# A gathered-expert decoder layer: the gates' exponential and its division one step later in each unit

## The reference, cut to what matters

```python
s1, i1 = lax.top_k(scores[:, :, :, 0, :], PEER_TOPK)
s2, i2 = lax.top_k(scores[:, :, :, 1, :], PEER_TOPK)
cand = (s1[..., :, None] + s2[..., None, :]).reshape(B, S, PEER_HEADS, PEER_TOPK * PEER_TOPK)
top_s, top_c = lax.top_k(cand, PEER_TOPK)
...
gates = jax.nn.softmax(top_s, axis=-1).astype(x.dtype)
...
ue = jnp.take(u_tab, idb, axis=0)
h = jnp.einsum('thkd,td->thk', ue, xb)
act = gb * jax.nn.gelu(h, approximate=False)
ve = jnp.take(v_tab, idb, axis=0)
return jnp.einsum('thk,thkd->td', act, ve)
```

## Time and profile before

| | us |
|---|---|
| median of 3 runs | 1428.41 |
| lowest and highest | 1425.42, 1432.09 |
| the profiled execution | 1430.31 |
| its span, first to last instruction | 1428.6 |
| busy: PE, DVE, ACT, POOL | 1132.4, 1078.3, 936.5, 562.6 |
| granted TensorE clock, mean share of full | 0.889 |

### The profile page before, as it was taken

The page is one execution under the profiler, slowest core; times in us unless marked ns, Lnnn a source line. Parts: engine busy times, 40 slices in busy tenths (PEclk is TensorE's granted clock), DMA queues, the critical chain, the costliest instruction groups (busy, mean ns, idle before and its releaser), DMA issues.

```text
span 1428.6 us, 19360 instructions
## 1 busy us (share of the span) xinstructions
PE 1132.4 (79%) x6804; PEld 882.6 (62%) x6804; DVE 1078.3 (75%) x2602; ACT 936.5 (66%) x1613; POOL 562.6 (39%) x535
## 2 busy tenths in 40 slices
PE   9999999988689877796646988877658776776666
PEld 4567777666676666675645557755556565555555
DVE  1488777668778886688757668888887788878867
ACT  2245677679878888766636666567666766667563
POOL 1044344334544344445324334444334343434341
PEclk9999999999889989899778987888788888888778
DMA  9799999999999999999999999999999999999994
GB/s 356 277 387 423 419 426 394 425 423 426 414 426 404 426 422 424 426 426 421 427 428 426 425 426 409 416 408 426 427 427 404 425 427 426 428 426 427 426 425 148
DMA packets 89787, 584.06 MB, mean 409 GB/s; under 512 B 9709, under 2 KB 15253, under 8 KB 22490
## 3 DMA queue, kind: packets, MB, share of 16 engines
q0 software_dynamic: 74288, 536.90, 89.9%
q1 hardware_dynamic: 15402, 45.92, 8.2%
HBM read 580.69 MB, written 2.10 MB: 408 GB/s over the span
## 4 chain that ended last, share of the span: by engine, by line
DMA 47%; PE 22%; DVE 18%; issue 7%; ACT 4%; POOL 2%; POOLq 0%; DVEq 0%; ACTq 0%
DMA arena<-in_uv,ids 47%; DVE arena L1819 9%; PE ps L1187 6%; PE ps L1082 2%; PE ps L1006 2%; PE ps L872 2%; POOL arena L658 2%; ACT arena L1445 2%; PE ps L702 1%; PE ps L692 1%; PE ps L685 1%; ACT actv L1438 1%; PE ps L949 0%; PE ps L942 0%; PE ps L769 0%
## 5 line engine op out<-in xcount | busy, mean ns | idle before, releaser
L658 POOL DMA_INDIRECT arena<-in_uv,ids x512 | 549.1, 1073 | 802.9 <-DVE hid L1819 527.8
L1187 PE MATMUL ps<-ident,arena 128*128 128x128 f32 x4076 | 613.9, 310 | 278.2 <-ACT arena L1445 277.1
L1187 PEld LDWEIGHTS ps<-ident,arena 128*128 128x128 f32 x4076 | 535.3, 160 | 378.2 <-ACT arena L1445 336.8
L1819 DVE CUSTOM_DVE_ANT_1 arena<-arena 128x1024 f32<-128x1024 f32 x384 | 468.4, 1224 | 195.4 <-DMA arena<-in_uv,ids 192.2
L1445 ACT ACTIVATE arena<-arena,actv 128x1024 f32<-128x1024 f32 x511 | 554.2, 1131 | 0.2
L1435 ACT ACTIVATE gel<-hid 128x2 f32<-128x2 f32 (+1 forms) x257 | 52.1, 203 | 378.6 <-DVE hid L1819 378.1
L1819 DVE CUSTOM_DVE_ANT_0 arena<-arena 128x1024 f32<-128x1024 f32 x128 | 155.5, 1225 | 64.9 <-DMA arena<-in_uv,ids 63.8
L1438 ACT ACTIVATE actv<-gel,gates 128x1 f32<-128x1 f32 x511 | 122.9, 287 | 8.4
L872 PE MATMUL ps<-arena 128*128 128x128 f32 x992 | 120.1, 281 | 0.0
L872 PEld LDWEIGHTS ps<-arena 128*128 128x128 f32 x992 | 118.0, 198 | 0.0
L1006 PE MATMUL ps<-arena 128*128 128x384 f32 x192 | 65.9, 486 | 0.0
(11 more groups left out here) (268 smaller groups left out, 1004.8 us busy)
## 6 DMA issues: line engine op xcount, KB each, us to landing
arena<-in_wq SPq DMA_DIRECT2D x10, 1024.0 KB, 9.3
arena<-in_uv,ids POOLq DMA_INDIRECT x519, 10.4
arena<-in_w_out SPq DMA_DIRECT2D x2, 2048.0 KB, 12.3
arena<-in_w_gate SPq DMA_DIRECT2D x1, 4096.0 KB, 16.8
arena<-in_w_out SPq DMA_DIRECT2D x3, 1024.0 KB, 13.9
arena<-in_w_k SPq DMA_DIRECT2D x4, 512.0 KB, 7.6
arena<-in_w_q SPq DMA_DIRECT2D x2, 1024.0 KB, 10.1
arena<-in_w_v SPq DMA_DIRECT2D x2, 1024.0 KB, 10.2
```

The lines of the kernel that those rows point to most:

```text
L658: nc.gpsimd.indirect_dma_start(out=row(u, c)[:, 0:n], out_offset=None, in_=a["uv"][:, :], in_offset=bass.IndirectOffsetOnAxis(ap=ids[:, u ...
L1187: i = mm(ps[:, run_bank(r) + k // 4, (k % 4) * P:(k % 4 + 1) * P], row(u, c)[:, D + k * P:D + (k + 1) * P], ident[:, :], is_transpose=True ...
L1819: v.tensor_tensor_reduce(out=r, in0=r, in1=x1[t], scale=1.0, scalar=0.0, op0=ALU.mult, op1=ALU.add, accum_out=hid[:, i, c:c + 1]).then_inc ...
```

## The change

Two conditions change, one on ACT and one on DVE. The exponential of unit u+1, for u from 1, comes in step 6 of unit u and not in step 5; the first unit's is as before (step 7 of unit 0). The division by the sum, for u from 1 to 30, comes in step 7 and not in step 6. With the exponential go its two table loads where nothing else needs them.

```diff
@@ -1478,7 +1478,7 @@
                 logs = [m for m in range(1, len(BATCHES)) if step == Z_AT[m] + TO_LOG]
                 exps = [m for m in range(1, len(BATCHES)) if step == Z_AT[m] + TO_EXP]
-                ranked = step % NG == (5 if step >= NG else 7) and step // NG + 1 < NU
+                ranked = step % NG == (6 if step >= NG else 7) and step // NG + 1 < NU
                 if logs or exps or ranked:
                     act.preload_act_table_set("natural_log_exp_and_others")
                 if ranked:
@@ -2032,7 +2032,7 @@
                             rank_rest(u + 1)
                         if g == (first + 4 if u else 5):
                             rank_ids(u + 1)
-                    if 0 < u < NU - 1 and g == 6:
+                    if 0 < u < NU - 1 and g == 7:
                         norm_gates(u + 1)
                     background(u * NG + g)
```

## The result

The changed kernel is slower by a little: ratio 1.0039, 95% interval 1.0030 to 1.0049, which is 5.6 us on 1428.6. The medians are 1435.16 us (22 runs) and 1428.64 us (22 runs). The interval lies clear of no change and within the 0.5% that the prediction called a measurement's limit. The forecast was 1429.5 us with a range of 1424 to 1437.

What follows compares the result with a forecast made beforehand. The prediction took DMA refilling a ring of row buffers as the bound. Losses of 0.4 (unit 2) and 0.7 us (unit 6) made 1431.4 us for the profiled execution; with the median 1.9 us lower, 1429.5 us, range 1424 to 1437.

Steps and rivals of the forecast that it cites:

- the forecast itself (0.74): The main case, against the three rivals: the change costs 0 to 4 us, chance 0.74.
- three signs of being wrong: DMA rate at 400 to 600 us down over a few GB/s; unit 6's gather used over 1.5 us later; plain units longer.
- Five more pairs of loads: ScalarE, about 200 to 590 us: 50 of each load instead of 45, 12.8 us more work; six units lose sharing.
- Plain units cost nothing: Units without shared loads: step 7 starts 1.2 us late in place of step 6's 1.0; the row buffers cover it, 0.
- The division: VectorE, end of a unit: waits for the later exponential, some 10 to 15 us in all instead of 4.9; cost 0.
- Rival (b): Division becomes the wait, holding up VectorE's dots and the gathers: 8.4 us over six units, 1436.8 us; chance 0.04.
- Unit 2: Step 23 starts 2.7 us late where TensorE is the bound; its rows end later, 0.4 us lost.
- Unit 6: Step 55's late rows delay a gather by 2.7 us; the queue gives back 2.0 us, 0.7 us lost.
- Step 62: Unit 7, priced as a plain unit: last rows 0.2 us later, their buffer asked for three rows later, counted 0.
- The order behind the copies: ScalarE, step 6: exponential and loads, 3.03 us, stand behind the next query's copy, priced at 0.36 us.
- Rival (a): Step 7's rows free buffers 2.7 us late in six units, DMA runs dry: 16.2 us, 1444.6 us; chance 0.13.
- Rival (c): Plain units free row buffers 1 us earlier and 4.9 us of division waits go: 1423.5 us; chance 0.09.

## Why the prediction came out as it did

The forecast, no change beyond 0.5% within a range of 1424 to 1437 us, held. The loss is real: 5.6 us, 4.3 to 7.0 by its interval, where 1.1 was worked out and the forecast itself (0.74) allowed 0 to 4. So the range held by the width that it had for scatter and for part of the rivals, which is some luck, and not by its sum. The interval also shows that the measurement told far less than the 0.5% that I had taken as its limit. Of the three signs of being wrong, two appear in the change's profile (408 GB/s at 400 to 600 us where it was 421; the gather of unit 6 used 3.4 us late) and neither in the trace with units 1 to 10 changed (417 GB/s, still a few lower; 1.2 us). Plain units did not get longer.

- **Five more pairs of loads, and which units get them:** right (50 of each line). The place of their cost, units 2 and 6 and not 3, 4, 9 and 10, was right: 5.0 us against 0.0 in the two kernels with extra pairs. Those pairs stand behind step 5, where they cost unit 2 more than the change does, so they show the place and not the change's sizes.
- **Plain units cost nothing:** right, by the kernel that changes units 11 to 30 alone and by the one with 24 extra loads.
- **The division:** right that it costs nothing by itself. Rival (b) fell with the kernel that takes its waits away. The waits were more than forecast, 25.3 us against 10 to 15.
- **Unit 2:** 0.4 us forecast, 0.7 to 0.8 in the three traces with this order.
- **Unit 6:** the term was too small. It read "2.0 us of the delay are queue that can be spent, and 2.7 - 2.0 = 0.7 us are lost". In two traces the delay at the gather was 2.9 us, 1.7 and 2.1 us of it came back, and the lag grew by 1.7 and 1.8 us: the mechanism held and the size was short by 1 us. In the change's profile the delay was 3.7 us, because squares that wait for TensorE stand ahead of the exponential, only 0.3 us came back, and 3.1 to 3.4 us were lost.
- **Step 62:** the term that was put at nothing. The prediction let late last rows cost 0 since "the row buffer behind it is asked for only three rows later". At the end of a tile the sums of these rows have a second reader, `add_run` on VectorE, and it now waits 0.58 to 0.83 us (3.44 in the change's profile). The lag grows there by 0.5 to 1.7 us (3.3).
- **The order behind the copies:** I placed the exponential "behind the copy of the next query" and priced only that copy's length. The copy and the squares wait for TensorE, up to 2.97 us in the change's profile. By the medians unit 18 does not pay for it, and step 62 at most 2.4 us.
- **Rival (a), late rows passed on in full:** its mechanism happened in part, in two of its six units and not in three or more. In most traces part of the delay came back, so the half of it that would have crossed 0.5% did not come.
- **Rival (c), a gain:** nothing of it, as its own counter-argument said.
- **The drain of "ScalarE: Activation LUTs" in the Trainium skill** (section "What ACT_TABLE_LOAD costs"): no row here shows it. In the kernel with extra pairs three loads in a row start at 921.34, 922.63 and 923.92, 1.29 us apart. The skill's rule to batch by table set (section "Table sets: the hidden batching unit") points the right way here, though by place and not by number: four loads cost 5.0 us, twenty-four cost none.

What stays open: the three places add up to 2.9 us (0.7 + 1.7 + 0.5) and 3.5 us (0.8 + 1.8 + 0.9) in the two other traces with the moved exponential and its loads, against 5.6 us (4.3 to 7.0) for the change and 3.7 us (2.1 to 5.3) for units 1 to 10. The loss by units 1 to 10 and by units 11 to 30 (about none) add up to 0.19%, less than the 0.39% of the whole; that gap is about as large as the three intervals together allow, so it may be chance, or the two halves add to each other. Unit 2 and unit 6 were not run apart with the exponential in step 6, and the part that is left without the added loads (0.18%, at least 0.04%) has a place and a candidate, step 62 and `add_run`, but no cause shown.

## What to carry to other kernels

In a ring that DMA bounds, ask of each added wait or instruction not how long it is but what stands behind it in that very stretch: 30.8 us of table loads were free where ScalarE had 2 us of idle per step, and four loads cost 5 us, 3.9 of them by the trace in the unit where TensorE was the bound. List every reader of what gets late: the row buffers had room, the sums of a finished tile had not. When a piece that shares its table loads with another is moved, count the pairs again. A repair that moves the delay to another waiter (the query copy here) gives nothing back. And where several kernels share a stretch of program, compare their traces there before a size is read from one of them.

## What the hardware showed that I had not expected

How much of a gather's delay the queue takes up differs between executions of the same program: a gather issued 3.7 us late was used 3.4 us late (8.50 us from issue to use) in one trace, and 2.9 and 1.2 us late (7.14 us) in another. And the same 32 products (128x128) took 3.74 us in one trace and 5.36 us in the other, with a granted clock of 1.00 and of 0.72 over the stretch.
